# Routing of a hierarchical MoE: choice by rank on VectorE, softmax weights and record addresses on GpSimd, two expert gathers ahead of the record scatters

## The reference

```python
def hier_moe(x, w_group, b_group, w_expert, b_expert, w_gate, w_up, w_down):
    xt = x.reshape(B_ * S, D)
    g_prob = jax.nn.softmax((xt @ w_group + b_group), axis=-1)
    g_w, g_idx = lax.top_k(g_prob, 1)
    e_logits_all = jnp.einsum('td,gde->tge', xt, w_expert) + b_expert
    e_logits = jnp.take_along_axis(e_logits_all, g_idx[:, None, None], axis=1)[:, 0]
    e_prob = jax.nn.softmax(e_logits, axis=-1)
    e_w, e_idx = lax.top_k(e_prob, EXPERT_TOPK)
    e_w = e_w / jnp.sum(e_w, axis=-1, keepdims=True)
    w_tok = g_w[:, None] * e_w
    ...
    for e in range(N_EXPERTS):
        h = jax.nn.silu(xt @ w_gate[e]) * (xt @ w_up[e])
        y = y + combine[:, e:e + 1] * (h @ w_down[e])

a = moba_attention(...); r = hgrn2(...)            # 8 + 8 heads x 64, 512 tokens
x = layer_norm(ALPHA * x + concat(a, r) @ w_o)
x = layer_norm(ALPHA * x + hier_moe(x))            # 4 groups x 4 experts, D 1024, D_EXPERT 512
```

## Time and profile before

| What | Value |
|---|---|
| Three runs | 615.7, 615.74, 617.25 us; median 615.74 |
| The profiled execution | 615.53 us, span 613.6 us |
| PE busy | 591.4 us, 96% of the span |
| DVE busy | 478.5 us, 78% |
| ACT busy | 373.4 us, 61% |
| POOL busy | 129.3 us, 21% |
| Chain that ended last | PE 92%, DVE 4% |

### The profile page before, as it was taken

The page is one execution under the profiler, slowest core; times in us unless marked ns, Lnnn a source line. Parts: engine busy times, 40 slices in busy tenths (PEclk is TensorE's granted clock), DMA queues, the critical chain, the costliest instruction groups (busy, mean ns, idle before and its releaser), DMA issues.

```text
span 613.6 us, 9635 instructions
## 1 busy us (share of the span) xinstructions
PE 591.4 (96%) x3627; PEld 475.8 (78%) x3627; DVE 478.5 (78%) x572; ACT 373.4 (61%) x401; POOL 129.3 (21%) x111
## 2 busy tenths in 40 slices
PE   8999999999999999999799999999999999999991
PEld 6878888888788668877588888888888888888880
DVE  3748598794577775546898989888888988888967
ACT  3659434431315984213478877877877787787745
POOL 0004222290000340000484443111110111111010
PEclk9999999999999999999899999999999999999997
DMA  9821133223306003975699999999999999999754
GB/s 325 299 98 57 63 130 111 95 71 78 72 1 206 2 2 125 422 271 211 239 375 420 404 363 389 392 388 391 409 404 389 389 389 389 399 410 397 269 172 137
DMA packets 42573, 155.77 MB, mean 254 GB/s; under 512 B 11955, under 2 KB 12163, under 8 KB 30252
## 3 DMA queue, kind: packets, MB, share of 16 engines
q1 hardware_dynamic: 37516, 138.40, 57.8%
q0 software_dynamic: 5024, 16.92, 10.6%
HBM read 139.96 MB, written 15.34 MB: 253 GB/s over the span
## 4 chain that ended last, share of the span: by engine, by line
PE 92%; DVE 4%; issue 1%; ACT 1%; DMA 1%; DVEq 0%; SPq 0%
PE psum L673 26%; PE psum L675 25%; PE psum L674 25%; PE psum L1072 2%; PE psum L791 2%; PE psum L931 2%; PE psum L908 2%; PE psum L1089 1%; PE psum L895 1%; PE psum L687 1%; DMA cst<-in_c_main 1%; PE psum L833 1%; PE psum L821 1%; PE psum L777 1%; DVE ring L2033 1%
## 5 line engine op out<-in xcount | busy, mean ns | idle before, releaser
L1810 DVE TENSOR_TENSOR w_lo<-ring,w_hi 128x2048 fp32r<-128x2048 f32 x95 | 216.8, 2299 | 23.3 <-ACT w_hi L1380 22.1
L673 PE MATMUL psum<-w_hi,act_hi 128*128 128x512 f32 x538 | 216.5, 402 | 0.8 <-DVE w_lo L1810 0.6
L675 PE MATMUL psum<-w_hi,act_lo 128*128 128x512 f32 x538 | 210.3, 391 | 0.0
L674 PE MATMUL psum<-w_lo,act_hi 128*128 128x512 f32 x538 | 210.0, 390 | 0.0
L1380 ACT ACTIVATE w_hi<-ring 128x2048 fp32r<-128x2048 f32 x96 | 182.2, 1917 | 25.0 <-PE psum L675 22.3
L673 PEld LDWEIGHTS psum<-w_hi,act_hi 128*128 128x128 f32 x538 | 101.3, 188 | 26.9 <-DVE w_lo L1810 4.7
L675 PEld LDWEIGHTS psum<-w_hi,act_lo 128*128 128x128 f32 x538 | 101.0, 188 | 21.9
L674 PEld LDWEIGHTS psum<-w_lo,act_hi 128*128 128x128 f32 x538 | 101.2, 188 | 19.0
L627 POOL DMA_INDIRECT acc_dram<-misc,slots x15 | 25.8, 1720 | 192.8 <-ACT misc L1430 178.8
L1228 ACT ACTIVATE w_hi<-ring 128x2048 fp32r<-128x2048 f32 x17 | 32.6, 1918 | 49.0 <-PE psum L675 47.3
L1539 DVE TENSOR_TENSOR w_lo<-ring,w_hi 128x2048 fp32r<-128x2048 f32 x17 | 39.8, 2344 | 23.0 <-ACT w_hi L1228 22.8
(11 more groups left out here) (254 smaller groups left out, 692.7 us busy)
## 6 DMA issues: line engine op xcount, KB each, us to landing
ring<-in_w_gate SPq DMA_DIRECT2D x32, 1024.0 KB, 19.8
ring<-in_w_up SPq DMA_DIRECT2D x32, 1024.0 KB, 19.6
ring<-in_w_down SPq DMA_DIRECT2D x32, 1024.0 KB, 19.9
ring<-in_w_in SPq DMA_DIRECT2D x13, 1024.0 KB
ring<-in_w_o SPq DMA_DIRECT2D x4, 1024.0 KB
acc_dram<-ring SPq DMA_DIRECT2D x5, 512.0 KB, 4.0
ring<-in_x SPq DMA_DIRECT2D x2, 1024.0 KB, 6.4
ring<-strip_dram SPq DMA_DIRECT2D x8, 256.0 KB, 4.9
```

What stands on the lines that cost most here:

```text
L673: pe.matmul(dst, lh, rh, start=first, stop=False, skip_group_check=True)
L674: pe.matmul(dst, lh, rl, start=False, stop=False, skip_group_check=True)
L675: return pe.matmul(dst, ll, rh, start=False, stop=last, skip_group_check=True)
L1810: dve.tensor_tensor(w_lo[:, v0 % WBUF, :], ring[:, slot, :], w_hi[:, v0 % WBUF, :].bitcast(F32), ALU.subtract).then_inc(s_lo, 1)
```

## The change

`first_max` goes. `ranks` (for two tiles at once) subtracts every logit of a four from every other, compares with a tie table (0, or the smallest normal float), and adds up: the number of logits that beat this one. Rank 0 is the best, rank below 1.5 the best two. Tiles 0 and 1 are ranked ahead of the last tile's residual, tiles 2 and 3 behind the last logits. The softmax input, the two choices, their products with group and position, the sums (as halving additions) and the addresses go to GpSimd, behind the first two gathers, each operation behind a wait for the one before. The exponential moves on ACT behind `e_hi` of expert 1. GpSimd finishes the sum of the exponentials, gathers experts 2 and 3, and then scatters all records. The reciprocal stands on DVE behind `elo(4)` and waits for GpSimd's sum. `elo(1)` moves ahead of `e_lo` of expert 0, the first expert's first four blocks run pass by pass, and the fillers are 29, 9 (new, ahead of the token lists) and 30.

```diff
@@ -85,8 +85,8 @@
-    c[:, C_W4:C_W4 + 4] = [4, 3, 2, 1]
-    c[:, C_E16:C_E16 + NE] = np.arange(NE)
+    c[:, C_TIE:C_TIE + 16] = [0 if i < j else np.finfo(np.float32).tiny for j in range(4) for i in range(4)]
+    c[:, C_E16:C_E16 + NE] = np.arange(NE) - NE
@@ -607,14 +611,53 @@
+    pooled = [2]
+    def then(ins):
+        pooled[0] += 1
+        ins.then_inc(s_pool, 1)
+        pool.wait_ge(s_pool, pooled[0])
+    def folded(v, n, op):
+        while n > 1:
+            n //= 2
+            then(pool.tensor_tensor(v(0, n), v(0, n), v(n, 2 * n), op))
+    pool.wait_ge(s_rneed, 1)
+    pooled[0] = 4
+    pool.wait_ge(s_pool, 4)
+    then(pool.tensor_tensor(r_x[:, :, 0:NG], r_l[:, :, 0:NG], r_top.broadcast_to((P, T, NG)), ALU.subtract))
+    then(pool.tensor_scalar(r_hot, r_rank[:, :, NG:NL], 0.5, None, ALU.is_lt))
+    then(pool.tensor_scalar(r_hot2, r_rank[:, :, NG:NL], 1.0, None, ALU.is_equal))
+    then(pool.tensor_tensor(four(r_sel[:, 0]), four(r_hot), group_four, ALU.mult))
+    then(pool.tensor_tensor(four(r_sel[:, 1]), four(r_hot2), group_four, ALU.mult))
+    then(pool.tensor_tensor(r_step, r_sel[:, 1], r_sel[:, 0], ALU.subtract))
+    then(pool.tensor_tensor(r_step, r_step, r_l[:, :, NG:NL], ALU.mult))
+    folded(lambda a, b: r_step[:, :, a:b], NE, ALU.add)
+    pool.tensor_copy(r_x[:, :, NG:NG + 1], r_step[:, :, 0:1]).then_inc(s_rneed, 1)
+    e16 = cst[:, C_E16:C_E16 + NE].rearrange("p (a e) -> p a e", a=1)
+    then(pool.tensor_scalar(r_pos, r_at1, float(NE), None, ALU.mult))
+    then(pool.tensor_tensor(r_pos, r_pos, e16.broadcast_to((P, T, NE)), ALU.add))
+    for k in range(2):
+        then(pool.tensor_tensor(r_sel[:, k], r_sel[:, k], r_pos, ALU.mult))
+    sel = r_sel.rearrange("p k i e -> p (k i) e")
+    folded(lambda a, b: sel[:, :, a:b], NE, ALU.add)
+    then(pool.tensor_copy(addr_i[:, :, :].rearrange("p k i -> p (k i)").rearrange("p (n a) -> p n a", a=1), sel[:, :, 0:1]))
+    pool.wait_ge(s_rexp, 1)
+    folded(lambda a, b: r_x[:, :, a:b], NG, ALU.add)
+    then(pool.tensor_scalar(r_q, r_x[:, :, NG:NG + 1], ALPHA, ALPHA, ALU.mult, ALU.add))
+    pool.tensor_tensor(r_gsum, r_x[:, :, 0:1], r_q, ALU.mult).then_inc(s_addr, 1)
...
+    pool.wait_ge(s_slots, 3)
+    gather(2)
+    gather(3)
...
+    then(pool.tensor_tensor(weight_of(rec_i[:, :, 1, 2:3]), weight_of(rec_i[:, :, 0, 2:3]), r_x[:, :, NG:NG + 1], ALU.mult))
...
-        if n == 5:
-            pool.wait_ge(s_slots, 3)
-            gather(2)
-        if n == 7:
-            gather(3)
@@ -1041,7 +1084,7 @@
-    keep_warm(32, 4)
+    keep_warm(29, 4)
@@ -1049,6 +1092,7 @@
+    keep_warm(9, 1)
@@ -1120,22 +1164,23 @@
-    keep_warm(24, 1)
+    keep_warm(30, 1)
...
-    pe.wait_ge(s_lo, MIX_UNITS + 1)
-    block = lambda k: (slice(k * P, (k + 1) * P), slice(k * DE, (k + 1) * DE))
-    for k in range(4):
-        xs, ws = block(k)
-        high(bank(2), e_hi[:, 0, xs], w_hi[:, 0, ws], w_lo[:, 0, ws], k == 0)
-    pe.wait_ge(s_xtlofirst, 1)
-    for k in range(4):
-        xs, ws = block(k)
-        last = pe.matmul(bank(2), e_lo[:, 0, xs], w_hi[:, 0, ws], start=False, stop=False, skip_group_check=True)
+    pe.wait_ge(s_hi, MIX_UNITS + 1)
+    passes = [(e_hi, w_hi), (e_hi, w_lo), (e_lo, w_hi)]
+    for n, (x, w) in enumerate(passes):
+        if n == 1:
+            pe.wait_ge(s_lo, MIX_UNITS + 1)
+        elif n == 2:
+            pe.wait_ge(s_xtlofirst, 1)
+        for k in range(4):
+            last = pe.matmul(bank(2), x[:, 0, k * P:(k + 1) * P], w[:, 0, k * DE:(k + 1) * DE], start=(n == 0 and k == 0), stop=False,
+                             skip_group_check=True)
@@ -1406,8 +1451,6 @@
-    act.wait_ge(s_rneed, 1)
-    act.activation(r_x, r_x, ACT.Exp).then_inc(s_rexp, 1)
@@ -1459,6 +1502,8 @@
+    act.wait_ge(s_rneed, 2)
+    act.activation(r_x, r_x, ACT.Exp).then_inc(s_rexp, 1)
@@ -1851,6 +1896,18 @@
+    def ranks(t0):
+        ls = r_l[:, t0:t0 + 2, :].rearrange("p t (g e) -> p (t g) e", e=4)
+        shape = (P, 2 * (1 + NG), 4, 4)
+        link(dve.tensor_tensor(r_beats, ls.rearrange("p s (a i) -> p s a i", a=1).broadcast_to(shape),
+                               ls.rearrange("p s (j a) -> p s j a", a=1).broadcast_to(shape), ALU.subtract))
+        tie = cst[:, C_TIE:C_TIE + 16].rearrange("p (a j i) -> p a j i", a=1, j=4)
+        link(dve.tensor_tensor(r_beats, r_beats, tie.broadcast_to(shape), ALU.is_ge))
+        link(dve.tensor_reduce(r_rank[:, t0:t0 + 2, :].rearrange("p t (g e a) -> p (t g) e a", e=4, a=1), r_beats, AX.X, ALU.add))
+    ranks(0)
@@ -1863,40 +1920,20 @@
-    def bc(ap, n):
-        return ap.broadcast_to((P, T, n))
...
-    w4 = cst[:, C_W4:C_W4 + 4].rearrange("p (a n) -> p a n", a=1)
-    def first_max(values, hot, top, first, n):
-        values, hot = values.rearrange("p t (g e) -> p (t g) e", e=4), hot.rearrange("p t (g e) -> p (t g) e", e=4)
-        link(dve.tensor_reduce(top, values, AX.X, ALU.max))
-        link(dve.tensor_tensor(hot, values, top.broadcast_to((P, n, 4)), ALU.is_equal))
-        link(dve.tensor_tensor(hot, hot, w4.broadcast_to((P, n, 4)), ALU.mult))
-        link(dve.tensor_reduce(first, hot, AX.X, ALU.max))
-        link(dve.tensor_tensor(hot, hot, first.broadcast_to((P, n, 4)), ALU.is_equal))
-    first_max(r_l, r_hot, r_top, r_first, T * (1 + NG))
-    link(dve.scalar_tensor_tensor(out=r_l2, in0=r_hot[:, :, NG:NL], scalar=-BIG, in1=r_l[:, :, NG:NL], op0=ALU.mult, op1=ALU.add))
-    first_max(r_l2, r_hot2, r_top2, r_first2, T * NG)
-    group = r_hot[:, :, 0:NG]
-    def in_group(dst, src):
-        four = lambda v: v.rearrange("p t (g e) -> p t g e", g=NG)
-        return dve.tensor_tensor(four(dst), four(src), group.rearrange("p t (g a) -> p t g a", a=1).broadcast_to((P, T, NG, EPG)), ALU.mult)
-    link(dve.tensor_tensor(r_both, r_hot[:, :, NG:NL], r_hot2, ALU.add))
-    in_group(r_msk, r_both).then_inc(s_mask, 1)
+    ranks(T // 2)
+    link(dve.tensor_scalar(r_group, r_rank[:, :, 0:NG], 0.5, None, ALU.is_lt))
+    dve.scalar_tensor_tensor(out=four(r_msk), in0=four(r_rank[:, :, NG:NL]), scalar=1.5, in1=group_four,
+                             op0=ALU.is_lt, op1=ALU.mult).then_inc(s_mask, 1)
...
+    dve.tensor_reduce(r_top, r_l[:, :, 0:NG], AX.X, ALU.max)
...
-    e16 = cst[:, C_E16:C_E16 + NE].rearrange("p (a e) -> p a e", a=1)
-    link(dve.scalar_tensor_tensor(out=r_at1, in0=pos, scalar=1.0, in1=r_msk, op0=ALU.add, op1=ALU.mult))
+    dve.scalar_tensor_tensor(out=r_at1, in0=pos, scalar=1.0, in1=r_msk, op0=ALU.add, op1=ALU.mult).then_inc(s_rneed, 1)
+    dve.wait_ge(s_rneed, 1)
@@ -1913,25 +1950,8 @@
-    tops = r_top.rearrange("p (t g) a -> p t (g a)", t=T)
-    link(dve.tensor_tensor(r_x[:, :, 0:NG], r_l[:, :, 0:NG], tops[:, :, 0:1].broadcast_to((P, T, NG)), ALU.subtract))
-    link(dve.tensor_tensor(r_d, r_top2.rearrange("p (t g) a -> p t (g a)", t=T), tops[:, :, 1:1 + NG], ALU.subtract))
-    link(dve.tensor_tensor(r_d, r_d, group, ALU.mult))
-    dve.tensor_reduce(r_x[:, :, NG:NG + 1], r_d, AX.X, ALU.add).then_inc(s_rneed, 1)
-    in_group(r_sel[:, 0], r_hot[:, :, NG:NL])
-    in_group(r_sel[:, 1], r_hot2)
-    link(dve.scalar_tensor_tensor(out=r_pos, in0=pos, scalar=float(NE), in1=e16.broadcast_to((P, T, NE)), op0=ALU.mult, op1=ALU.add))
-    r_sel_flat, r_t16_four = r_sel, r_t16.rearrange("p (k i) e -> p k i e", k=2)
-    link(dve.tensor_tensor(r_t16_four, r_sel_flat, r_pos.rearrange("p (a i) e -> p a i e", a=1).broadcast_to((P, 2, T, NE)), ALU.mult))
-    link(dve.tensor_reduce(r_adr, r_t16, AX.X, ALU.add))
-    dve.tensor_copy(addr_i[:, :, :].rearrange("p k i -> p (k i)"), r_adr.rearrange("p n a -> p (n a)")).then_inc(s_addr, 1)
-    dve.wait_ge(s_rexp, 1)
-    link(dve.tensor_reduce(r_gsum, r_x[:, :, 0:NG], AX.X, ALU.add))
-    link(dve.tensor_scalar(r_q, r_x[:, :, NG:NG + 1], ALPHA, ALPHA, ALU.mult, ALU.add))
-    link(dve.tensor_tensor(r_gsum, r_gsum, r_q, ALU.mult))
-    link(dve.reciprocal(weight_of(rec_i[:, :, 0, 2:3]), r_gsum))
-    dve.tensor_tensor(weight_of(rec_i[:, :, 1, 2:3]), weight_of(rec_i[:, :, 0, 2:3]), r_x[:, :, NG:NG + 1], ALU.mult).then_inc(s_addr, 1)
...
+    elo(1, 0)
@@ -1969,7 +1989,6 @@
-    elo(1, 0)
@@ -1977,6 +1996,8 @@
+    dve.wait_ge(s_addr, 1)
+    dve.reciprocal(weight_of(rec_i[:, :, 0, 2:3]), r_gsum).then_inc(s_addr, 1)
```

More of the change, by code:

```diff
@@ L66 @@
 C_SCAN = C_MASK + 64 * (1 + len(LEVELS))
-C_W4 = C_SCAN + SEQ
-C_E16 = C_W4 + 4
+C_TIE = C_SCAN + SEQ
+C_E16 = C_TIE + 16
 C_REC = C_E16 + NE
@@ L307, in build, with four @@
         r_msk = msk_b[:, :].rearrange("p (i e) -> p i e", i=T)
-        r_l, r_hot, r_top, r_first = rcol(T, NL), rcol(T, NL), rcol(T * (1 + NG), 1), rcol(T * (1 + NG), 1)
-        r_l2, r_hot2, r_top2, r_first2 = rcol(T, NE), rcol(T, NE), rcol(T * NG, 1), rcol(T * NG, 1)
-        r_x, r_d, r_both, r_gsum, r_gw, r_q = rcol(T, NG + 1), rcol(T, NG), rcol(T, NE), rcol(T, 1), rcol(T, 1), rcol(T, 1)
+        r_l, r_group, r_hot, r_hot2, r_top = rcol(T, NL), rcol(T, NG), rcol(T, NE), rcol(T, NE), rcol(T, 1)
```

(5 more changed lines are left out.)

## The result

The changed kernel took 623.79 us (median of 4 runs, 623.05 to 624.81), the kernel before 616.50 us (4 runs, 615.7 to 617.64): 1.0115 times as long, 95% interval 1.0098 to 1.0132. The profiled execution has a span of 622.6 us and an own time of 624.44 us, 9.0 us of span over the one before.

A forecast was written before the change was run, and what follows sets the result against it. PE bounds the kernel (92% of the chain that ended last). 615.5 + 9.9 for the late slots + 0.8 for slow clock = 626.2, about 626 us, early 2.9 us included; own range 622 to 631, overall 614 to 633.

The forecast's parts named there:

- the wait: ACT's output of expert 1 waits for the late slots, passed whole to PE before unit 16: 9.9 us later.
- the clock's price: PE's second stand, 4 us: its slow clock may cost 0 to 1.7 us; 0.8 added.
- T: End of GpSimd's 25 small operations, the sum DVE's reciprocal waits for: 319.7 us, between 316 and 323.5.
- Ranking: On DVE up to the mask: 3.17 us become 1.3, gain 1.9 us (bounds 2.1 and 1.4).
- Start of the first expert: PE before 307 us: full clock, gather issued 295.3, landing 299.1; 2.9 us gained with unit 1's wait gone.
- The port: Shared by DVE and GpSimd: whatever GpSimd starts inside a `w_lo` waits for its end, about 0.85 us beyond it.
- The gather that was let pass: First gather, issued 0.18 us ahead of `w_lo` 0, assumed not held by it; if caught, it costs 2.3 us.
- The chain: 25 small dependent operations on GpSimd, 0.5 us each, 12.5 us if nothing blocks; ends 0.34 and 0.72 each.
- the size of DVE's wait: DVE waits behind `w_lo` 4 (313.4) for GpSimd's sum until 319.7; PE stands 7 us ahead of step 1.
- That rule: Forecast called wrong if DVE waits under 2 us at the reciprocal; alternatively, if slots arrive before ACT needs them.
- The rival that had only this wait: DVE waits for GpSimd's sum, but record issues are not caught and slots come in time: 621 us, chance 0.2.
- The slots: Records leave late, so slots reach GpSimd 36.5 us after its chain ends (bounds 26 and 40); ACT waits 4 us more.

The follow-up runs named there:

- reciprocal behind: Changed kernel with the reciprocal, and DVE's wait for GpSimd's sum, moved behind expert 0's hidden product: 623.61 us, ratio 1.0109 to the kernel before.
- weights back: Changed kernel with softmax, addresses and reciprocal back on DVE, exponential and record order as before; ranking and fillers stay: 615.12 us, ratio 0.9971.
- both early traces: Changed kernel with the reciprocal behind expert 0's hidden product, 623.61 us, and changed kernel with 14 fillers instead of 29, 622.16 us.

## Why the prediction was right, and where not

The forecast of 626 us had the sign and the place, and the path from the slots to PE; the time came out 2.2 us lower, in its own range of 622 to 631. Part of that closeness is luck: of the 10.7 us that it added, the wait was 3.8 us too large and the clock's price 1.6 too small. And it made T, the end of GpSimd's chain, the sole cause. The run with the records behind both gathers has no such chain, and its slots are the latest of all (353.17): gather 2's wait for its lists (until 315.65) and the two gathers ahead of the first record are enough without T.

**Ranking.** Three operations over 160 elements took 0.33, 0.33 and 0.32 us with 0.03 between, as estimated, and the whole from 291.31 to the mask 1.29 us, forecast 1.3. The mask came 1.64 us earlier, forecast 1.9, because its first operation began 0.24 us later than before.

**Start of the first expert.** The 2.9 us did not appear in the profiled execution. The full clock from 297 was right, but the low clock had moved to 289.5, where I had not looked for it, and the fillers there outlasted the mask by 1.6 us (292.83 to 294.46). Where the clock was full (reciprocal behind, weights back), the gather left at 295.3 as forecast, but took 4.8 to 4.9 us to the transposes, not 3.8, with SP's load beside it, so these came at 300.1 instead of 299.1. The weights-back kernel turned this early start into 1.8 us of time.

**The port.** The gather that was let pass passed (1.05 us); the second was caught (1.97). The chain's first operation, of 16 elements, took 1.40 us up to the end of `w_lo` 1; the one at 303.89 took 2.35 us, 0.12 us into a `w_lo` of 2.28.
On this point the Trainium skill (SBUF — State Buffer, Who interferes with whom) says that a DVE instruction with two SBUF inputs contends with a GpSimd instruction that reads SBUF, as an exclusive lock, and that `tensor_tensor` was not seen to stall DMA. On the first the rows agree in one direction: GpSimd is held until a `w_lo` ends, while the two `w_lo` from 297.12, begun under the first gather's issue, still took 4.49 us. On the second the measurement differs, since under `w_lo`, a `tensor_tensor`, a record's issue took up to 2.92 us in the changed kernel against 0.96 free.

**The chain, and the step that failed: the size of DVE's wait.** I took 0.5 us for each operation. Where no `w_lo` held them, they took 0.38 to 0.39 (`tensor_scalar`, 64 elements), 0.30 to 0.32 (`tensor_tensor`, 64) and 0.19 to 0.20 (4 elements), with 0.08 us between them, a third to a half of the gap I took from DMA issues. T was 316.6, not 319.7. DVE waited 1.50 us, less than the 2 us below which I had called the forecast wrong, and PE stood 1.74 us ahead of step 1 instead of 7, without a fall of the clock. That rule was badly chosen: the forecast rested on T above 310, and with the reciprocal moved neither the first scatter (321.91 in both early traces) nor the median changes beyond the interval. The rival that had only this wait (621 us) named the wrong one of the two.

**The slots.** They came at T + 35.8, forecast T + 36.5. Of this, the gathers, the product and the eight issues took 24.4 (forecast 26.2), and the landing and the read 11.4 (forecast 10.3). ACT was 6.1 us later than before, forecast 9.9; the difference of 3.8 is 3.1 from T and 0.7 from the slots. PE stood 5.5 us there, not 4, since it had lost less before. The wait passed to PE whole (6.13 of 6.13).

**The clock.** I added 0.8 us for it. The stand of 5.5 us was followed by about 6 us at half speed, 8.54 - 6.13 = 2.4 us. By the measured sizes, 6.1 + 2.4 = 8.5 us of the 9.0 between the spans; the other 0.5 came later and is not traced. The medians differ by 7.3 us only: the profiled execution of before is at the low end of its runs and that of after in the upper half of its own.

## What to carry to other kernels

When work moves to another engine, or only changes its order there, follow each product (here the records, then the slots, then one scalar for ACT) to its first reader, and compare the arrival with the slack there (5.9 us of slack, 12 us of delay). Then test the order and the moved work apart: here the order alone gave the whole loss, and the forecast had put it down to the moved chain. A local wait on the path need not count, when a later one absorbs it. Fillers that are meant to keep the clock up delay what stands behind them when they themselves run at half clock; fewer of them narrowed the spread of the times, but in one execution the clock then fell a little later instead.
